# A three-block transformer stack on one core: stage changes of 512 tokens done in two token halves

## The reference, cut to what matters

```python
x   = x   + 0.5 * m_lat[:, 2] * swiglu(modulate(rms_norm_2(x), m_lat[:, 0], m_lat[:, 1]), ffn_in[l, 0], ffn_out[l, 0])
ctx = ctx + 0.5 * m_ctx[2] * swiglu(modulate(rms_norm_2(ctx), m_ctx[0], m_ctx[1]), ffn_in[l, 0], ffn_out[l, 0])
h_lat = modulate(rms_norm_2(x), m_lat[:, 3], m_lat[:, 4])
h_ctx = modulate(rms_norm_2(ctx), m_ctx[3], m_ctx[4])
...                       # even_mixer or odd_mixer, then x = x + m_lat[:, 5] * o_lat
x = x + 0.5 * m_lat[:, 8] * swiglu(modulate(rms_norm_2(x), m_lat[:, 6], m_lat[:, 7]), ffn_in[l, 1], ffn_out[l, 1])

def rms_norm_2(x):     return x * rsqrt(mean(x * x, axis=-1) + EPS)
def modulate(h, shift, scale): return h * (1.0 + scale) + shift
def swiglu(h, w_in, w_out):
    gate, up = split(h @ w_in, 2)          # 1024 -> 2 x 2816
    return (silu(gate) * up) @ w_out       # 2816 -> 1024
```

## Time and profile before

| what | us |
|---|---|
| median of 3 runs | 2589.05 |
| lowest and highest run | 2589.02, 2594.82 |
| the profiled execution, its own time | 2589.12 |
| span of its trace, first to last instruction | 2587.3 |
| PE busy / DVE busy / ACT busy | 2430.0 / 1456.0 / 902.9 |
| mean granted clock of PE, as a share of full speed | 0.975 |

### The profile page before, as it was taken

How to read it: one execution, slowest core, us unless ns; L and a number is a source line. 1 busy time by engine, 2 the same in 40 slices (tenths; PEclk the granted TensorE clock), 3 DMA queues, 4 the chain that set the end, 5 groups by cost and what they waited for, 6 DMA issues and landing times.

```text
span 2587.3 us, 42406 instructions
## 1 busy us (share of the span) xinstructions
PE 2430.0 (94%) x17862; PEld 1975.0 (76%) x17862; DVE 1456.0 (56%) x2331; ACT 902.9 (35%) x1522; POOL 76.5 (3%) x148
## 2 busy tenths in 40 slices
PE   8998999999999988877778999999999999999998
PEld 6687778688887766766776788877688877777997
DVE  5656565655554567666554555544655544475553
ACT  2341132523222446543233422222422222455543
POOL 0000000000000000000000000000000000000000
PEclk9999999999999999997988999999999999999999
DMA  8236526344344311000003343444343443212553
GB/s 306 94 130 212 179 98 211 140 145 138 139 139 147 133 51 48 1 4 20 4 4 114 106 146 132 145 138 147 122 146 133 144 138 131 85 50 92 186 180 130
DMA packets 55916, 310.95 MB, mean 120 GB/s; under 512 B 5936, under 2 KB 9392, under 8 KB 28080
## 3 DMA queue, kind: packets, MB, share of 16 engines
q1 hardware_dynamic: 32944, 224.75, 24.5%
q0 software_dynamic: 20736, 75.51, 9.0%
q10 hardware_dynamic: 2048, 7.98, 0.8%
HBM read 307.16 MB, written 1.05 MB: 119 GB/s over the span
## 4 chain that ended last, share of the span: by engine, by line
PEld 43%; PE 28%; issue 13%; DVE 11%; ACT 4%; PEldq 0%; DVEq 0%; DMA 0%; ACTq 0%; SPq 0%
PEld bank L1503 14%; PEld bank L1496 14%; PEld bank L1499 13%; PE bank L1345 5%; PE bank L1342 2%; PE bank L1546 2%; PE bank L1404 2%; PE bank L1420 2%; PE bank L1158 1%; PE bank L1161 1%; PE bank L1165 1%; PE bank L1232 1%; PE bank L1291 1%; ACT hn L2023 1%; DVE ms L2474 1%
## 5 line engine op out<-in xcount | busy, mean ns | idle before, releaser
L2487 DVE TENSOR_TENSOR w_lo<-ring,w_hi 128x1024 fp32r<-128x1024 f32 (+1 forms) x195 | 232.5, 1192 | 440.7 <-ACT w_hi L1986 440.7
L1496 PE MATMUL bank<-ffn_x_hi,w_hi 128*128 128x512 f32 x984 | 388.7, 395 | 0.0
L1499 PE MATMUL bank<-ffn_x_lo,w_hi 128*128 128x512 f32 x984 | 388.7, 395 | 0.0
L1503 PE MATMUL bank<-ffn_x_hi,w_lo 128*128 128x512 f32 x984 | 388.7, 395 | 0.0
L1986 ACT ACTIVATE w_hi<-ring 128x1024 fp32r<-128x1024 f32 (+1 forms) x195 | 200.5, 1028 | 281.7 <-PE bank L1499 271.0
L2418 DVE SCALAR_TENSOR_TENSOR ms<-mod_rows,c_silu 128x1024 f32<-128x1024 f32 x200 | 243.9, 1220 | 1.3
L1496 PEld LDWEIGHTS bank<-ffn_x_hi,w_hi 128*128 128x128 f32 x984 | 184.4, 187 | 45.3
L1499 PEld LDWEIGHTS bank<-ffn_x_lo,w_hi 128*128 128x128 f32 x984 | 184.4, 187 | 45.2
L1503 PEld LDWEIGHTS bank<-ffn_x_hi,w_lo 128*128 128x128 f32 x984 | 184.4, 187 | 45.1
L1496 PE MATMUL bank<-ffn_h_hi,w_hi 128*128 128x512 f32 x528 | 213.4, 404 | 0.0
L1503 PE MATMUL bank<-ffn_h_hi,w_lo 128*128 128x512 f32 x528 | 208.6, 395 | 0.0
(11 more groups left out here) (500 smaller groups left out, 4735.8 us busy)
## 6 DMA issues: line engine op xcount, KB each, us to landing
ring<-in_stream SPq DMA_DIRECT2D x211, 1024.0 KB, 4.8
mod_rows<-in_mod_stream POOLq DMA_DIRECT2D x144, 512.0 KB, 3.8
one_const<-in_one ACTq DMA_DIRECT2D x1, 1665.0 KB, 14.4
mix_const<-in_two ACTq DMA_DIRECT2D x1, 1440.0 KB, 6.3
win_const<-in_win ACTq DMA_DIRECT2D x1, 1216.0 KB, 5.1
x<-in_x SPq DMA_DIRECT2D x4, 256.0 KB, 4.5
c_silu<-in_c SPq DMA_DIRECT2D x1, 1024.0 KB, 10.3
x<-in_x SPq DMA_DIRECT2D x1, 1024.0 KB, 26.5
```

The source lines that it names most:

```text
L1496: mm = pe.matmul(bank[:, 0:tok], w_high, hi, start=k == 0, stop=False)
L1499: mm = pe.matmul(bank[:, 0:tok], w_high, lo, start=False, stop=False)
L1503: mm = pe.matmul(bank[:, 0:tok], w_low, hi, start=False, stop=last)
L2487: V.tensor_tensor(low[:, 0:h.nk, :], raw_half(h), high[:, 0:h.nk, :].bitcast(F32), ALU.subtract).then_inc(sem("w_split"), 1)
```

## The change

At the five changes with 512 tokens the work goes by token halves (`token_halves`): first tokens 0 to 255 through a step, then 256 to 511.

- `gated_add` of the last chunk signals after its first half (`half_updated`), and `square` of that chunk is two instructions of 256 columns.
- `sum_squares` uses two banks, one for each half, with one product of 256 columns for each.
- `root_of_sums` and the refinement (`inverse_root`) work on one half. ACT takes both first roots one behind the other; DVE refines the first half, and the second half when `ROOT_AT` = 5 chunks of the first have been begun.
- The barrier that stood before the norm stage now stands behind ACT's roots and DVE's first refinement. PE's `keep_busy` comes after it and has 5 products.
- Scaling, shift, high and low part are one instruction for each chunk and half: 16 steps for 8, all of the first half before all of the second. ACT splits one weight half before the first chunk and one more after each of chunks 0 and 1.
- `ffn` begins three weight halves in the first chunks for two; the third lags by `THIRD_LAG` = 4 chunks in the first token half. Products there have 256 columns, twice as many as before for each weight half. The `blend` values go by halves too.
- The fourth weight half is split earlier in ACT's and DVE's order.

The change with 256 tokens keeps its order of instructions. The core of the diff:

```diff
             def sum_squares(c, tok):
 
+                halves = token_halves(tok)
                 if c == 0:
-                    sums.append(take_bank())
-                    sums_base[0] = tally("squares", KC)
-                bank, full = sums[-1]
+                    sums[:] = [take_bank() for _ in halves]
+                    sums_base[0] = tally("squares", KC - 1 + len(halves))
                 pe.wait_ge(sem("squares"), sums_base[0] + c + 1)
-                mm = pe.matmul(bank[:, 0:tok], ones, squares[c % 4][:, 0:tok], start=c == 0, stop=c == KC - 1)
+                for t, cols in enumerate(halves):
+                    bank, full = sums[t]
+                    if c == KC - 1 and t:
+                        pe.wait_ge(sem("squares"), sums_base[0] + KC + 1)
+                    mm = pe.matmul(bank[:, 0:SEQ], ones, squares[c % 4][:, cols], start=c == 0, stop=c == KC - 1)
...
+                keep_busy(taken[0][0], WARM if tok == SEQ else WARM_HALVES)
+                for t, cols in enumerate(token_halves(tok)):
+                    late = THIRD_LAG if t == 0 and begun == 3 else 0
+                    for at in range(KC + late):
+                        if at < KC:
+                            wait_normed(at, t)
+                            for n in range(2):
+                                if t == 0 and at == 0:
+                                    enter(n)
+                                chunk(n, t, cols, at)
+                        if begun == 3 and at >= late:
+                            if t == 0 and at == late:
+                                enter(2)
+                            chunk(2, t, cols, at - late)
...
+                by_token = token_halves(tok) if kind in ("split", "mixed") else [slice(0, tok)]
+                for t, cols in enumerate(token_halves(tok)):
+                    root_of_sums(t, cols)
+                if len(by_token) > 1:
+                    barrier()
...
-                        for k in range(tok // SEQ):
-                            cols = slice(k * SEQ, (k + 1) * SEQ)
-                            last = nc.scalar.activation(hn[:, kc, cols], hn[:, kc, cols], ACT.Identity,
-                                                        scale=modv[:, layer, v + 1, kc, k:k + 1],
-                                                        bias=modv[:, layer, v, kc, k:k + 1])
-                        link(last)
-                        x_hi = (ph5 if kind == "split" else mixed[layer])["x_hi"]
-                        nc.scalar.activation(x_hi[:, kc, 0:tok], hn[:, kc, 0:tok], ACT.Copy).then_inc(sem("x_hi_ready"), 1)
+                    for k, cols in enumerate(by_token):
+                        for kc in range(KC):
+                            act.wait_ge(sem("x_scaled"), b + k * KC + kc + 1)
+                            link(nc.scalar.activation(hn[:, kc, cols], hn[:, kc, cols], ACT.Identity,
+                                                      scale=modv[:, layer, v + 1, kc, k:k + 1],
+                                                      bias=modv[:, layer, v, kc, k:k + 1]))
+                            nc.scalar.activation(x_hi[:, kc, cols], hn[:, kc, cols], ACT.Copy).then_inc(sem("x_hi_ready"), 1)
+                            if kind == "split" and k == 0 and early + kc < EARLY:
+                                split_high(halves_of[2 * which[0] + (which[1] > 0)], early + kc, 0)
...
+                if len(by_token) > 1:
+                    barrier()
+                for n, (kc, cols) in enumerate(chunks):
+                    if n == ROOT_AT and len(by_token) > 1:
+                        inverse_root(1, by_token[1])
+                    V.tensor_tensor(hn[:, kc, cols], x[:, kc, cols], rstd[:, cols], ALU.mult).then_inc(sem("x_scaled"), 1)
+                    if n == 0 and kind == "mixed":
+                        split_low(parts_of[which[0]], 0, mixed_half(which[0]))
+                    elif n in (0, 2, 4) and kind == "split":
+                        split(halves, n // 2)
+                    if n:
+                        low_part(n - 1)
+                low_part(len(chunks) - 1)
```

271 lines of the change are left out of this document (143 added, 128 removed).

## The result

| | kernel before | changed kernel |
|---|---|---|
| median | 2590.66 us (11 runs) | 2608.67 us (11 runs) |
| lowest and highest run | 2588.82, 2602.77 | 2600.78, 2621.83 |
| the profiled execution | 2589.12 us, span 2587.3 | 2604.09 us, span 2602.3 |
| ratio to before | | 1.0072, 95% interval 1.0057 to 1.0087 |

A forecast was written before the change was run, and what follows sets the result against it. PE, busy 94% of the span, was taken as the bound, with only its pauses to gain. Delays 0.9 + 1.1 + 2.5 + 1.3 = 5.8, with the clock 7.0, on 2589.12 gave 2596 us; 8-in-10 range 2584 to 2603.

The forecast's parts named there:

- the layout of the steps: 512-token changes: scaling at +4.40, second root from +12.4, ACT idle 2.7, 0.94 per ACT step, fourth weight half at +29.6.
- 0.45, 0.45, 1.1, 2.5 and 1.3: Forecast delays in us: ffn(0, 1) and ffn(1, 0) 0.45 each, ffn(0, 0) 1.1, blend(0) 2.5, blend(1) 1.3.
- The rule that asks for 512 elements: Skill's fixed cost per VectorE and ScalarE instruction; paid in full, both blend entries end 1.1 later each, time 2598.
- Two more banks for sums: nothing, they are read before the idle products need them: At the 512-token changes, using two more PSUM banks for the halved sums was to cost 0.
- the clock, 1.2: Three ffn entries: granted-clock falls after the second pause cost up to 1.7 each; bounds 0 and 5.1, taken as 1.2.
- what stands behind the fourth weight half: ffn entries: fifth weight half done at about 34.9, needed at 35.3, still covered; no later cost counted.
- The moved barrier: Behind the first roots, DVE last: 0.10, with ACT's first weight split, PE's idle products and DVE's scaling queued behind.
- The early start: Rival: 2.1 earlier first useful product stays at each of five changes, 10.5 less, 2578.5; chance 0.11.
- absorbed: Rival: blend(0)'s 2.5 may shrink behind waiting attention and ffn entries come out even; +1 to +2, 2590.5; chance 0.23.
- the rival: Clock falls into dense products at each ffn entry, after the pause from +11.7 to +15.1; about 2601, chance 0.21.

The follow-up runs named there:

- the kernel with the late bank: Changed kernel, but PE takes the third weight half's bank where that half starts, not ahead of the idle products; median 2601.66 us, ratio 1.0056.
- the kernel with the third half alone: Kernel before, with three weight halves begun in the 512-token ffn entries, third two chunks behind, fourth's split earlier, all else whole; median 2606.76 us, ratio 1.0068.

## Why the prediction was wrong, point by point

**Right: the layout of the steps.** Scaling, first root, second root, ACT's gap, the 0.94 per step, 144 products at 0.12: all stood within 0.1 of the forecast, and with them 0.45, 0.45, 1.1, 2.5 and 1.3 came out as 0.51, 0.54, 1.09 (in the kernel with the late bank), 2.70 and 1.22. Their sum was 5.8 and measured 6.1. That `ffn(0, 1)` and `ffn(1, 0)` met their marks this closely was in part luck of the one execution: no fall of the clock came in their second pause, where the kernel with the late bank had two. The rule that asks for 512 elements, which the prediction weighed, would have made the two `blend` entries 1.1 later each; they were 2.70 and 1.22, so the pace in the row, 0.94, was the right price.

**The step that failed: "Two more banks for sums: nothing, they are read before the idle products need them".** I took it from the five changes as if they were one. At `ffn(0, 0)` the third of the three banks is the second sum's, which is read only when the second root is made, 8 us behind the barrier. It cost 5.2, shown by the kernel that takes the bank later. No duration was wrong here; a wait was missing, and the order of PE's program had it in a row of its own, whose list holds the banks of both sums, where at the other changes it holds that of the first at most.

**A term that was mis-sized: the clock, 1.2.** I priced only falls at the `ffn` entries. In the profiled execution of the changed kernel there was none at `ffn(0, 1)`, and that at `ffn(1, 0)` met idle products and cost nothing. The 1.74 in the stretch with the recurrence and the 1.02 ahead of the first change fit the 3.4 us more at half clock in each. They also lie inside what single executions differ by: in the nine traces that have neither the long fall nor idle products ahead of the recurrence, the stretch of the 1.74 takes 532 to 541. So they are not shown to be a steady cost of the change. The upper half of the runs took 5 to 18 more than the profiled one. In two other kernels' traces one long fall in the recurrence makes up the height, 15.6 and 18.8 (576.1 and 579.3 for 560.5). For the changed kernel itself this was not seen, since both of its profiled executions are from the lower runs. What is on record fits it: the four runs from 2618 up have a mean granted clock of 0.961 to 0.964, the five lowest 0.970 to 0.973, and 38 us more at half clock would lower it by 0.007. The fall into dense products behind the second pause, which I priced at up to 1.7, is real, though not in this trace: the kernel with the late bank has it at +15.7 and +14.7 in two `ffn` entries, at 1.2 to 1.3 each, and four more of the kernels have it once or more. What I did not price was a long fall hundreds of us behind the entries.

**A cost I held for nothing: what stands behind the fourth weight half.** 0.40 and 0.33 behind the marks of `ffn(0, 1)` and `ffn(1, 0)`. Not tried further.

**The moved barrier.** I counted it as 0.10 and named what queues behind it, PE's idle products among them, but not that PE stands still for the time. With three products in that wait the median of the eight lower runs stands 6.2 above the kernel before of its sitting, for 8.5 without them, some 2 us.

**The rivals.** The early start did not carry through: the mark came 0.5 later. Nothing was absorbed. The clock did fall into useful work, in this trace only outside the five changes, in the kernel with the late bank at two of the three `ffn` entries, as the rival has it.

**What stays open.** What lifts the upper runs of the changed kernel, beyond the fit above. Why all six runs of the kernel with the third half alone stand some 25 us above the five with six idle products added (the chips differ as well), and why none of the 87 runs of the kernel before went above 2602.77, while the recurrence has the same instructions in the same order. The traces show one regularity: in the two executions with the long fall it begins 0.9 and 1.0 us behind the end of PE's 3.07 us pause; in one with 10 us at half clock, 1.05 behind; in the eleven others it begins 0.6 to 1.1 ahead of that end (seven) or 1.7 to 2.3 behind it (four) and is over within 7 us. What in a kernel moves that place from run to run was not found, and no run here was made to settle it.

## What to carry to other kernels

When an edit takes more of a ring (banks, slots), read for each place where the ring is used which piece the next taker gets and who gives it back; the same code met five times gave four answers of "nothing" and one of 5 us. Compare kernels timed in different sittings by the kernel that both had beside them: here 3 of an apparent 5 us were the sitting's. A barrier moved to suit one engine moves every engine's queue, and an engine that only waits may need its idle work on the near side of it. Where a third piece of work is at hand, let the engine that starves take it: that one part of the change, with six idle products ahead of the recurrence, is the faster kernel in the five runs that it had.
